# A step of a hybrid decoder on one core: the gates of one dense tile are scattered into a table in DRAM while the experts are selected, and two heads' sample tokens share a tile

## The reference

```
q = (xb @ w_q).reshape(blk, PEER_HEADS, 2, PEER_HALF)
s = jnp.einsum('thcd,hcnd->thcn', q, sub_keys).astype(jnp.float32)
s_top, i_top = lax.top_k(s, PEER_TOPK)
cand_s = (s_top[:, :, 0, :, None] + s_top[:, :, 1, None, :]).reshape(blk, PEER_HEADS, -1)
cand_e = (i_top[:, :, 0, :, None] * N_KEYS + i_top[:, :, 1, None, :]).reshape(blk, PEER_HEADS, -1)
best_s, best_pos = lax.top_k(cand_s, PEER_TOPK)
expert = jnp.take_along_axis(cand_e, best_pos, axis=-1)
gate = jax.nn.softmax(best_s, axis=-1)
act = jax.nn.gelu(jnp.einsum('td,thkd->thk', xb, u[expert]).astype(jnp.float32), approximate=False)
return jnp.einsum('thk,thkd->td', (gate * act).astype(xb.dtype), v[expert])
```

## Time and profile before

| | us |
|---|---|
| median of three runs | 5518.75 |
| the profiled execution | 5513.6 |
| its span, first to last instruction | 5511.7 |
| layer 0 selection, from 962.8 (first load) to 1246.06 (last VectorE instruction) | 283 |
| layer 0 build, from there to the first product at 1383.78 | 138 |
| layer 0 dense and sparse loop, to about 2520 | 1136 |
| TensorE, VectorE, GpSimd busy in the span | 4426.1, 3161.7, 1966.3 |

### The profile page before, as it was taken

One profiled execution on the slowest core, in us unless ns is written; L12 is line 12 of the kernel. 1 busy time (PEld: TensorE's weight loads), 2 busy tenths in 40 slices (PEclk: granted clock), 3 DMA queues, 4 the chain that ended last, 5 costly groups with the idle time before them and its releaser, 6 DMA issues. The chain is left out here.

```text
span 5511.7 us, 54596 instructions
## 1 busy us (share of the span) xinstructions
PE 4426.1 (80%) x19590; PEld 3192.4 (58%) x19590; DVE 3161.7 (57%) x6991; ACT 986.4 (18%) x1972; POOL 1966.3 (36%) x1548
## 2 busy tenths in 40 slices
PE   7988678828988888887886899866837988888886
PEld 5466447626655555554555788744625655555554
DVE  1314531698576667776119433243698577777775
ACT  0112310105111111111013222100105211111111
POOL 0000310120566666663003433120120565666663
PEclk9975769969999999998888888757968999999998
DMA  2320121203999999997120000112203899999998
GB/s 87 85 72 1 32 82 66 69 0 110 355 409 409 409 410 409 409 409 265 48 73 16 1 1 1 22 41 80 71 0 105 334 409 409 409 409 409 409 409 311
DMA packets 426733, 1109.97 MB, mean 201 GB/s; under 512 B 71740, under 2 KB 178973, under 8 KB 426006
## 3 DMA queue, kind: packets, MB, share of 16 engines
q0 software_dynamic: 184320, 671.17, 30.7%
q1 hardware_dynamic: 242150, 435.38, 22.4%
HBM read 1062.95 MB, written 46.08 MB: 201 GB/s over the span
## 5 line engine op out<-in xcount | busy, mean ns | idle before, releaser
L617 POOL DMA_INDIRECT fg_ug<-in_peer_u,f_idx x320 | 402.2, 1257 | 385.5 <-DVE fg_act_in L725 315.9
L617 POOL DMA_INDIRECT gg_ug<-in_peer_u,g_idx x320 | 385.3, 1204 | 359.6 <-DVE gg_act_in L725 298.7
L743 DVE SCALAR_TENSOR_TENSOR gg_xacc<-gg_vg,gg_wgt,gg_xacc 128x1024 f32<-128x1024 f32 x320 | 411.2, 1285 | 139.5 <-DMA gg_vg<-in_peer_v,g_idx 130.1
L872 PE MATMUL gg_out<-gg_dv,gg_gl 128*128 128x512 f32 x1024 | 467.2, 600 | 25.1 <-DVE gg_gl L713 24.8
L863 PE MATMUL fg_hid<-f_hT,fg_uT 128*128 128x256 f32 x2048 | 484.9, 392 | 0.0
L863 PE MATMUL gg_hid<-g_hT,gg_uT 128*128 128x256 f32 x2048 | 478.7, 388 | 0.0
L872 PE MATMUL fg_out<-fg_dv,fg_gl 128*128 128x512 f32 x1024 | 463.9, 596 | 12.7 <-DVE fg_gl L713 12.7
L743 DVE SCALAR_TENSOR_TENSOR fg_xacc<-fg_vg,fg_wgt,fg_xacc 128x1024 f32<-128x1024 f32 x320 | 411.9, 1287 | 92.5 <-DMA fg_vg<-in_peer_v,f_idx 82.4
L725 DVE CUSTOM_DVE_ANT_0 gg_ug<-gg_ug,gg_px 128x1024 f32<-128x1024 f32 x320 | 391.6, 1227 | 115.7 <-DMA gg_ug<-in_peer_u,g_idx 114.3
L624 POOL DMA_INDIRECT gg_vg<-in_peer_v,g_idx x320 | 368.5, 1152 | 204.9 <-DVE gg_xacc L743 135.2
L725 DVE CUSTOM_DVE_ANT_0 fg_ug<-fg_ug,fg_px 128x1024 f32<-128x1024 f32 x320 | 391.1, 1225 | 73.4 <-DMA fg_ug<-in_peer_u,f_idx 72.7
(11 more groups left out here) (593 smaller groups left out, 7327.2 us busy)
## 6 DMA issues: line engine op xcount, KB each, us to landing
fg_du<-in_peer_u SPq DMA_DIRECT2D x128, 512.0 KB, 9.0
fg_dv<-in_peer_v SPq DMA_DIRECT2D x128, 512.0 KB, 6.8
gg_du<-in_peer_u SPq DMA_DIRECT2D x128, 512.0 KB, 9.0
gg_dv<-in_peer_v SPq DMA_DIRECT2D x128, 512.0 KB, 6.8
awg_wt<-in_mix_w_out SPq DMA_DIRECT2D x4, 2048.0 KB, 7.5
fs_wt<-in_peer_w_q SPq DMA_DIRECT2D x8, 1024.0 KB, 5.6
scratch_gates<-fg_late SPq DMA_DIRECT2D x32, 256.0 KB, 2.6
fg_gates<-scratch_gates SPq DMA_DIRECT2D x16, 512.0 KB, 8.9
```

Source lines behind the costliest of these rows:

```text
L617: pool.indirect_dma_start(out=ug[:, n % NSLOT, :], out_offset=None, in_=u_rows, in_offset=bass.IndirectOffsetOnAxis(ap=index(n), axis=0)). ...
L743: dve.scalar_tensor_tensor(xacc[:, r, :], vg[:, g % NSLOT, :], wgt[:, s % 2, k:k + 1], xacc[:, r, :], ALU.mult, ALU.add).then_inc(v_done, 1)
L872: last = pe.matmul(out[:, r, 512 * c:512 * c + 512], gl[:, b % 2, r * P:(r + 1) * P], dv[:, b % 2, 512 * c:512 * c + 512], start=(b == 0), ...
```

## The change

It has four parts.

1. The gates of tile 2 (`PUT_TILE`) are no longer built from one-hots. There is a table in DRAM for each layer with one number for each pair of key numbers and token (16384 by 128, 8 MB). GpSimd adds tile 2's gates into it during the selection with indirect transfers: one for each of the 16 picks of a head, 128 numbers of 4 bytes each, one per token (`scatter`). The first 8 of head h-1 stand ahead of head h's lookups, the other 8 behind them. Ahead of the first 8, GpSimd waits for the addresses (`addr_done`, from `finish`) and until all transfers of the head before have landed; each of the other 8 waits for the one 8 places before it. `finish` makes the addresses in two more small instructions.
2. Both tables are zeroed once, in layer 0's mixer, on SP's queue ahead of the stores of keys and values (`kv_rows_out`, while the prompt's attention runs).
3. The build runs over the 128 tokens of tile 3 alone. Its table fits in SBUF whole, so `late`, its writes and its reads go. In the loop tile 2's gates come from DRAM in 32 pieces of 256 KB (`gates_put`, a ring of two), and `product` has two instructions, one for each tile.
4. The heads come in the order 0, 4, 1, 5, 2, 6, 3, 7. In every second turn the sample tile holds two heads, one in each half, and in the other turns VectorE, ScalarE and GpSimd work on 4 tiles and not 5; the two copies to the upper half go. The queries are kept for four heads. The scores of the first head are computed right behind the keys, and those of the second behind the third head's queries.

```diff
+ORDER = [0, 4, 1, 5, 2, 6, 3, 7]
+PACK = len(TILES) - 1
+
+
+def tiles_in(j):
+    return PACK + j % 2
+
...
+NPUT = 8
+PUT_TILE = 2
+def puts_before(layer, h):
+
+    return (layer * PH + h) * TOPK // NPUT
...
-                    for i, (t0, m) in enumerate(TILES):
+                    parts = [(i, 0, P, h) for i in range(PACK)]
+                    if h % 2:
+                        parts += [(PACK, 0, NS, h - 1), (PACK, NS, NS, h)]
+                    for i, p0, m, j in parts:
+                        t0 = TILES[i][0]
                         for c in range(2):
-                            last = pe.matmul(sc[0:m, i, c, :], qT[:, h % 2, c, t0:t0 + m], keysT[:, 2 * h + c, :],
-                                             start=True, stop=True)
+                            last = pe.matmul(sc[p0:p0 + m, i, c, :], qT[:, j % 4, c, t0:t0 + m],
+                                             keysT[:, 2 * ORDER[j] + c, :], start=True, stop=True)
...
-                for h in range(PH):
+                queries(0)
+                keys()
+                scores(0)
+                for h in range(1, PH):
                     queries(h)
-                    if h:
+                    if h > 1:
                         scores(h - 1)
-                    else:
-                        keys()
                 scores(PH - 1)
...
-                    act.activation(s_sb[0:64, h % 2, :, :, :], sc[0:64, 0:n, :, :], ACT.Copy)
-                    act.activation(s_sb[64:P, h % 2, 0:n - 1, :, :], sc[64:P, 0:n - 1, :, :], ACT.Copy).then_inc(s_done, 1)
+                    nt = tiles_in(h)
+                    act.activation(s_sb[:, h % 2, 0:nt, :, :], sc[:, 0:nt, :, :], ACT.Copy).then_inc(s_done, 1)
...
+                def scatter(h, ks):
+                    for k in ks:
+                        n = k % NPUT
+                        if k >= NPUT:
+                            pool.wait_ge(put[n], 16 * (puts_before(layer, h) + k // NPUT))
+                        pool.indirect_dma_start(
+                            out=table, out_offset=bass.IndirectOffsetOnAxis(
+                                ap=idx[:, PUT_TILE, TOPK * h + k:TOPK * h + k + 1], axis=0),
+                            in_=sel[:, PUT_TILE, 2, h, k:k + 1], in_offset=None, compute_op=ALU.add
+                            ).then_inc(put[n], 16)
+
+                def scatter_first(h):
+                    pool.wait_ge(addr_done, h + 1)
+                    if h == 0:
+                        pool.wait_ge(table_zero, 32)
+                    if layer or h:
+                        for n in range(NPUT):
+                            pool.wait_ge(put[n], 16 * puts_before(layer, h))
+                    scatter(h, range(NPUT))
+
                 for h in range(PH):
+                    nt = tiles_in(h)
+                    if h:
+                        scatter_first(h - 1)
                     for a in range(2):
                         pool.wait_ge(hit_done, 2 * h + a + 1)
-                        pool.tensor_tensor(hit[:, a, :, :, :], hit[:, a, :, :, :],
-                                           bc(itopf[:, h % 2, :, a, None, :], [P, n, TOPK, TOPK]), ALU.mult
+                        pool.tensor_tensor(hit[:, a, 0:nt, :, :], hit[:, a, 0:nt, :, :],
+                                           bc(itopf[:, h % 2, 0:nt, a, None, :], [P, nt, TOPK, TOPK]), ALU.mult
                                            ).then_inc(look_done, 1)
+                    if h:
+                        scatter(h - 1, range(NPUT, TOPK))
+                scatter_first(PH - 1)
+                scatter(PH - 1, range(NPUT, TOPK))
...
-                    dve.tensor_tensor(idx[:, :, TOPK * h:TOPK * (h + 1)], sel[:, :, 0, h, :], sel[:, :, 1, h, :], ALU.add)
+                    dve.tensor_tensor(idx[:, 0:nt, TOPK * h:TOPK * (h + 1)], sel[:, 0:nt, 0, h, :], sel[:, 0:nt, 1, h, :], ALU.add)
+                    own(dve.scalar_tensor_tensor(at[:, :], sel[:, PUT_TILE, 1, h, :], float(N_EXPERTS), sel[:, PUT_TILE, 0, h, :],
+                                                 ALU.mult, ALU.add))
+                    dve.tensor_scalar(idx[:, PUT_TILE, TOPK * h:TOPK * (h + 1)], at[:, :], token, float(-layer * N_EXPERTS),
+                                      ALU.add, ALU.add).then_inc(addr_done, 1)
...
+                    nt = tiles_in(h)
+                    tiles = [(i, c) for i in range(nt) for c in range(2)]
...
-PACK = len(TILES) - 1
-UNITS = [(i, h) for i in range(GTILES) for h in range(PH)] + [(PACK, h) for h in range(PH // 2)]
+UNITS = [(i, h) for i in range(GTILES) for h in range(PH)] + [(PACK, h) for h in range(1, PH, 2)]
+BTOK = DTOK - P
+NBG = BTOK // GB
+SB = 4
+TB0 = 1 + 2 * (GTILES + 1)
...
-        gates = ph.sb("gates", [P, NQ, NTG, QI, TG])
-        late = ph.sb("late", [P, 2, NQ, QI, TG])
+        gates = ph.sb("gates", [P, NBLK, BTOK])
+        put_rows = ph.sb("put_rows", [P, 2, SB, P])
...
+        by_key = table.rearrange("(j i t) o -> j i (t o)", j=N_KEYS, i=N_KEYS)
...
-                def gates_late(q, p):
-                    n = NTG // 4
-                    if p == 0:
-                        for c in range(2):
-                            sp.wait_ge(late_out[c], 16 * NTG // 2)
-                        sp.wait_ge(pr_done, QI * (q + 1))
-                    sp.dma_start(gates[:, q, n * p:n * (p + 1), :, :].rearrange("p g i t -> p g (i t)"),
-                                 g_dram[:, q, n * p:n * (p + 1), :]).then_inc(late_in[p], 16)
+                def gates_put(q):
+                    if q >= 2:
+                        sp.wait_ge(pr_done, SB * (q - 1))
+                    sp.dma_start(put_rows[:, q % 2, :, :], by_key[:, SB * q:SB * (q + 1), :]).then_inc(put_in[q % 2], 16)
...
-                sp.dma_start(idx[NS:P, PACK, 0:NPAIR // 2], idx[0:NS, PACK, NPAIR // 2:NPAIR]).then_inc(pair_in, 16)
-                sp.dma_start(sel[NS:P, PACK, 2, 0:PH // 2, :], sel[0:NS, PACK, 2, PH // 2:PH, :]).then_inc(pair_in, 16)
-                for g in range(NTG):
-                    sp.wait_ge(ev_done, GATE0 + 2 * (g + 1))
-                    sp.dma_start(g_dram[:, :, g, :], late[:, g % 2, :, :, :].rearrange("p q i t -> p q (i t)")
-                                 ).then_inc(late_out[g % 2], 16)
+                for n in range(NPUT):
+                    sp.wait_ge(put[n], 16 * puts_before(layer, PH))
+                gates_put(0)
+                gates_put(1)
                 for b in range(NBLK):
-                    if QI <= b < QBLK + 4 and b % QI < 4:
-                        gates_late(b // QI - 1, b % QI)
+                    if b >= SB and b % SB == 1 and b // SB + 1 < NBLK // SB:
+                        gates_put(b // SB + 1)
                     if b + 2 < NBLK:
...
                 def one_hots():
-                    for t in range(DTOK):
+                    for t in range(BTOK):
...
                 def product(b):
-                    q, i = b % QBLK // QI, b % QI
+                    q, i = b // SB, b % SB
                     dve.wait_ge(gl_done, b + 1)
                     if b == 0:
-                        dve.wait_ge(ev_done, GATE0 + NGB)
-                    if b >= QBLK and i == 0:
-                        for p in range(4):
-                            dve.wait_ge(late_in[p], 16 * (q + 1))
-                    g = gl[:, b % 2, :].rearrange("p (g t) -> p g t", t=TG)
-                    dve.tensor_tensor(g, g, gates[:, q, :, i, :], ALU.mult).then_inc(pr_done, 1)
+                        dve.wait_ge(ev_done, GATE0 + NBG)
+                    if i == 0:
+                        dve.wait_ge(put_in[q % 2], 16 * (q // 2 + 1))
+                    dve.tensor_tensor(gl[:, b % 2, 0:P], gl[:, b % 2, 0:P], put_rows[:, q % 2, i, :], ALU.mult)
+                    dve.tensor_tensor(gl[:, b % 2, P:DTOK], gl[:, b % 2, P:DTOK], gates[:, b, :], ALU.mult
+                                      ).then_inc(pr_done, 1)
...
                 def gates_out():
-                    for j in range(NGB):
-                        n = GATE0 + j
-                        g, t = GB * j // TG, GB * j % TG
-                        made = pt[:, n % 2, :, :]
+                    for j in range(NBG):
                         act.wait_ge(oh_used, j + 1)
-                        act.activation(gates[:, :, g, :, t:t + GB].rearrange("p q i t -> p t q i"),
-                                       made[:, :, 0:QBLK].rearrange("p t (q i) -> p t q i", i=QI), ACT.Copy)
-                        if t == 0 and g >= 2:
-                            act.wait_ge(late_out[g % 2], 16 * (g // 2))
-                        act.activation(late[:, g % 2, :, :, t:t + GB].rearrange("p q i t -> p t q i"),
-                                       made[:, :, QBLK:P].rearrange("p t (q i) -> p t q i", i=QI), ACT.Copy
-                                       ).then_inc(ev_done, 1)
+                        act.activation(gates[:, :, GB * j:GB * (j + 1)].rearrange("p i t -> p t i"),
```

(16 more changed lines are left out.)

136 lines of the change are left out of this document (66 added, 70 removed).

## The result

The changed kernel is slower: 5633.87 us, the median of four runs (5627.32 to 5649.24), against 5523.39 for the kernel before in four runs (5513.37 to 5538.72). The ratio is 1.0202, 95% interval 1.0168 to 1.0235: slower beyond doubt, by about 2%. The profiled execution took 5627.3 us, 113.7 more than the one before.

| stage | layer 0 before, after | layer 1 before, after | forecast |
|---|---|---|---|
| selection | 283.6, 390.9: +107.3 | 280.7, 387.7: +107.0 | +30.1 |
| build | 136.8, 68.4: -68.4 | 136.8, 68.6: -68.2 | -67.0 |
| loop | 1188.7, 1205.3: +16.6 | 1187.6, 1207.0: +19.4 | 0 |

What follows compares the result with a forecast made beforehand. VectorE bounds selection and build, DMA the loop; GpSimd then paces selection at 28.45 us a head. Selection +30.1, build -67.0: -36.9 a layer, -73.8 both, 5513.6 to 5439.8, plus 5.15: 5445 (chance 0.63; range 5415 to 5490, with rivals 5400 to 5600).

Steps and rivals of the forecast that it cites:

- The build: Build on VectorE: half of 256 tokens go (57.8 us) and waits behind late's writes (9.2), saving 67.0 us a layer.
- The first addresses: Selection: the first head's finish ends at 1057.1 us, and from there GpSimd has addresses.
- the landing: GpSimd in the selection: one wait per head for all transfers of the head before, 2.6 us.
- The price of a transfer: GpSimd in the selection: 1.24 us per adding transfer, taken from the gather, so 19.84 us a head for 16.
- The deciding point: Price of 1.53 us a transfer, at which the selection's growth equals the 67 us that the build saves.
- Rival 1: Adding transfers are slow, handled or landing one after the other: 5673 us, or 5634 at 1.98 a transfer; chance 0.20.
- VectorE's 26.0 us a head: VectorE in the selection: mean of 27.83 us for a five-tile turn and 24.16 for a four-tile turn.
- The prediction's estimate of 0.2 us a transfer on VectorE: Selection: blocking between VectorE's small instructions and the first 8 transfers costs some 0.2 us each, where there is room.
- The loop: Long loop, full of DMA: 8 MB of gates read as before, in 32 pieces; lasts 1136 us as before.
- rival 3: Smaller pieces of 2 KB a row and the second product lengthen the loop by 37 us a layer: 5517; chance 0.07.
- The second product instruction: Loop: 20 us of VectorE a layer, hidden beside a DMA limit with 338 us to spare.
- the zeroing: 16.8 MB written on SP's queue near 380 us, taking 63 us before a block ending near 559: cost nothing.

Runs made afterwards that it cites:

- lookups_first: half_puts with GpSimd's two lookups ahead of the 8 transfers instead of behind them: 5423.2 us, layer 0's selection 292.8 us.
- half_puts: The changed kernel with only the first 8 of a head's 16 transfers made: 5506.3 us, layer 0's selection 325.3 us.
- plain_write: The changed kernel with its 128 transfers a layer writing into the table without adding: 5491.9 us, layer 0's selection 315.8 us.
- long_split: long_runs with each row read as two runs of 2 KB from two places: loops 1202.7 and 1205.5 us, whole 5688.93 us.
- long_runs: The changed kernel reading 16 pieces of 512 KB in 4 KB runs, one-hot ring 4 instead of 8: loops 1186.8 and 1191.9 us, whole 5658.26 us.
- one_product: The changed kernel with a block's product as one instruction of 256 columns again: loops 1208.6 and 1201.7 us, whole 5637.68 us.

## Why the prediction was wrong

- **The build** (-67.0 forecast, -68.4 and -68.2 measured): right. The 12.7 us of waits went to 3.1; ScalarE's one copy of 512 numbers took 1.06 us and waited for TensorE, so VectorE stays the last.
- **The first addresses** (1057.1, measured 1054.42) and **the landing** (2.6, measured 2.17): right. The 0.74 for the first transfer behind a wait did not show (1.55 at 1093.88), and the lookups took 6.30 and 5.21, not 5.76 and 4.61; behind plain writes they took 5.75 and 4.67. Together, all that is not price was 8.05 us a head (37.65 less 16 x 1.85), where the sum has 8.61.
- **The price of a transfer** is the step that failed: "I take 1.24, since the instruction has the same count of addresses". Measured 1.85. What the nearest row, the gather, lacked was the addition: 0.59 us a transfer on GpSimd. Put into the prediction's own formula, 1057.1 + 7 x 8.61 + 128 x 1.85 = 1354.2, where the last transfer ended at 1349.0 and the build's first instruction started at 1351.8; the step is worth 78 us a layer. The deciding point, 1.53, was passed.
- **Rival 1** came true by its price alone. Its other half, landings one after the other as the pace, did not: a transfer lands 3.0 us after its issue (median) and the next goes out after 1.85, and layer 0's 128 transfers wait for landings 8 times, 15.5 us in all. That its 5634, for a price of 1.98, is the measured time is chance: the price was lower, and the loop, left at zero, made up for it.
- **VectorE's 26.0 us a head** was right for VectorE alone (26.2 in lookups_first) and wrong for where the change puts the lookups. The forecast saw that the 8 transfers push them beside the next head's search, and priced that at a shorter lookup; what it left out is VectorE's side, 5 us a head (31.3 in half_puts). That did not cost the changed kernel, where GpSimd is later still. At a price of 1.24 VectorE and not GpSimd would have set the pace, at 28.2 (plain_write, at 1.26): the forecast's 28.45 would have been met for another reason. The prediction's estimate of 0.2 us a transfer on VectorE rests on one one-hot of 0.50; the gather of 0.94 shown with it lies in VectorE's wait, but others beside one-hots took 0.93 and 0.94 as well.
- **The loop** (0 forecast, +16.6 and +19.4 measured): wrong. "The bytes are the same" held, their cost did not: runs of 2 KB in place of 4 KB cost some 15 us a layer (long_split against long_runs) in a loop without slack. This was rival 3's mechanism at half the size that it needed to decide. A smaller slip beside it: the reads of before stood in blocks 16 to 67, not in the second half.
- **The second product instruction** and **the zeroing** cost nothing that shows, as forecast: one_product changed nothing, and the two writes of 8 MB land 23.4 and 43.8 us after their issue (the row's 33.6 is their mean), long before 559. Layer 0's selection began no later (960.9, before 962.8), though with the mixers' scatter of some 20 us a small cost would be hidden.

Two terms carry the miss: 2 x 78 for the price and 36.0 for the loops take 5445 to 5637, against 5633.87; the 3 us that are left are within the runs' spread.

## What to carry to other kernels

A row that had the same shape but not the same operation gave a lower bound here, not a price: when one number decides the sign (here 1.53 against 1.24), double it in thought before betting on it, or measure it alone first. When work is moved in a queue, ask for both engines what will stand beside it at the new place. In a stretch where the DMA engines are full, "the same bytes" is not the same time: compare the length of the contiguous runs too.

## What was not expected of the hardware

An indirect transfer with 128 addresses occupies GpSimd 0.94 us as a gather, 0.96 as a write and 1.55 as an addition; with 64 addresses a plain write takes 0.89 and an addition 1.40, so half as many addresses are hardly cheaper. Beside two elementwise products on GpSimd a VectorE cast of 128 columns took 6.2 us, as long as they did, where one of 160 columns has 0.24 alone; Max8 beside them kept its pace. Reads of 8 MB beside a full DMA load cost 17 to 23 us in runs of 4 KB and 36 to 38 in runs of 2 KB, and the short runs' loss comes in single stretches, not as a steady lower rate.
